# The first norm of a two-model kernel: x over two DMA queues, squares on two engines, the sum over tiles on VectorE

## The reference

```python
def rms_norm(x, g):
    xf = x.astype(F32)
    y = xf * lax.rsqrt(jnp.mean(xf * xf, axis=-1, keepdims=True) + NORM_EPS)
    return (y * g.astype(F32)).astype(x.dtype)

def first_block(x, norm_mix_g, w_in, ...):
    h = x
    for layer in range(DEPTH):
        u = rms_norm(h, norm_mix_g[layer])
        p = u @ w_in[layer]
        p_a, p_b, p_c, p_gate = _split(p, (A_COLS, B_COLS, C_COLS, GATE_COLS))
        ...
```

## Time and profile before

| | us |
|---|---|
| median of three runs | 2533.5 (2531.13 to 2535.11) |
| the profiled execution | 2517.57 |
| its span, first to last instruction | 2516.1 |
| TensorE busy in the span | 2304.6 (92%) |
| VectorE busy | 1596.2 (63%) |
| ScalarE busy | 1178.8 (47%) |

### The profile page before, as it was taken

The page is one execution under the profiler, slowest core; times in us unless marked ns, Lnnn a source line. Parts: engine busy times, 40 slices in busy tenths (PEclk is TensorE's granted clock), DMA queues, the critical chain, the costliest instruction groups (busy, mean ns, idle before and its releaser), DMA issues.

```text
span 2516.1 us, 45037 instructions
## 1 busy us (share of the span) xinstructions
PE 2304.6 (92%) x19087; PEld 2076.5 (83%) x19087; DVE 1596.2 (63%) x2425; ACT 1178.8 (47%) x1717; POOL 0.2 (0%) x4
## 2 busy tenths in 40 slices
PE   7889788899988887988998989999989999999998
PEld 7669788899976777888998979998977788887776
DVE  5537776677763687576775656555654444568886
ACT  5234534455552355355554435445333434456665
POOL 0000000000000000000000000000000000000000
PEclk9999898999999999899998989999987999999999
DMA  5674333355446533253553414554312555569895
GB/s 201 224 257 157 113 106 105 130 183 191 139 173 261 197 118 116 86 175 121 193 192 100 134 59 168 185 190 137 118 34 84 184 176 183 190 237 324 321 330 197
DMA packets 118634, 427.06 MB, mean 170 GB/s; under 512 B 13344, under 2 KB 16160, under 8 KB 118304
## 3 DMA queue, kind: packets, MB, share of 16 engines
q1 hardware_dynamic: 116544, 422.34, 48.9%
q10 hardware_dynamic: 1888, 1.84, 0.2%
HBM read 423.08 MB, written 1.05 MB: 169 GB/s over the span
## 4 chain that ended last, share of the span: by engine, by line
PE 77%; DVE 14%; ACT 4%; issue 2%; DMA 2%; ACTq 0%; SPq 0%; DVEq 0%
PE bank L764 76%; DVE w_low L2176 4%; DVE arena L2208 4%; DMA ring<-in_weights 1%; DVE arena L2217 1%; DVE y_mix L2208 1%; ACT w_high L1672 1%; DVE arena L2678 1%; PE bank L1562 1%; ACT arena L1935 1%; DVE small L2676 0%; DVE arena L2214 0%; DVE arena L2212 0%; DVE arena L2227 0%; ACT arena L1880 0%
## 5 line engine op out<-in xcount | busy, mean ns | idle before, releaser
L2176 DVE TENSOR_TENSOR w_low<-ring,w_high 128x1024 fp32r<-128x1024 f32 x700 | 820.1, 1220 | 146.8 <-ACT w_high L1672 146.7
L764 PE MATMUL bank<-u_high,w_high 128*128 128x256 f32 x2576 | 743.0, 288 | 30.0 <-DVE u_low L2208 23.3
L1672 ACT ACTIVATE w_high<-ring 128x1024 fp32r<-128x1024 f32 x700 | 696.0, 1050 | 134.3 <-PE bank L764 128.0
L764 PE MATMUL bank<-u_low,w_high 128*128 128x256 f32 x2576 | 735.1, 285 | 0.0
L764 PE MATMUL bank<-u_high,w_low 128*128 128x256 f32 x2576 | 734.3, 285 | 0.0
L764 PEld LDWEIGHTS bank<-u_high,w_high 128*128 128x128 f32 x2576 | 499.7, 194 | 42.5 <-issue 39.5
L764 PEld LDWEIGHTS bank<-u_low,w_high 128*128 128x128 f32 x2576 | 499.7, 194 | 0.1
L764 PEld LDWEIGHTS bank<-u_high,w_low 128*128 128x128 f32 x2576 | 498.9, 194 | 0.0
L764 PE MATMUL bank<-arena 64*64 64x64 f32 (+8 forms) x4488 | 258.3, 253 | 78.8 <-DVE arena L2217 22.8
L764 PEld LDWEIGHTS bank<-arena 64*64 64x64 f32 (+3 forms) x4488 | 218.9, 154 | 124.7 <-issue 66.5
L764 PE MATMUL bank<-w_high,u_high 128*128 128x256 f32 (+1 forms) x480 | 166.5, 347 | 5.1 <-DVE w_low L2176 5.1
(11 more groups left out here) (281 smaller groups left out, 3091.1 us busy)
## 6 DMA issues: line engine op xcount, KB each, us to landing
ring<-in_weights SPq DMA_DIRECT2D x534, 512.0 KB, 4.5
ring<-in_moe SPq DMA_DIRECT2D x264, 512.0 KB, 5.3
const<-in_const SPq DMA_DIRECT2D x1, 2619.0 KB, 16.2
x_res<-in_x SPq DMA_DIRECT2D x2, 512.0 KB, 4.8
out<-x_res ACTq DMA_DIRECT2D x2, 512.0 KB, 3.0
const<-in_par ACTq DMA_DIRECT2D x1, 462.0 KB, 3.4
params<-in_par ACTq DMA_DIRECT2D x1, 247.0 KB, 7.9
small<-in_pos SPq DMA_DIRECT2D x1, 128.0 KB, 16.0
```

The lines of the kernel that those rows point to most:

```text
L764: return pe.matmul(out, lhsT, rhs, start=start, stop=stop, skip_group_check=loose)
L1672: act.activation(WH[:, ORDER.slot[cut], :], weights("s", cut), Copy).then_inc(s_hi, 1)
L2176: dve.tensor_tensor(WL[:, b, :], weights("s", cut), WH[:, b, :].bitcast(f32), SUB).then_inc(s_lo, 1)
```

## The change

The first half of x goes out on ScalarE's queue, ahead of `cond`; the second stays first on SyncE's queue. ScalarE squares tiles 0 to 3 in one instruction of 1024 elements a partition, VectorE squares tiles 4 to 7 in one. VectorE adds the two halves (1024 elements), folds the sum twice more (512, 256), and TensorE sums over the partitions with two matmuls instead of 16. The waits for `params` move: on VectorE to behind the low halves of units 0 and 1, on ScalarE to behind the norm. ScalarE cuts the high halves of units 0 and 1 ahead of the root and that of unit 2 behind it. VectorE makes the reciprocal between the low halves of units 1 and 2. The stage has steps of its own (`first`); layer 1 keeps `mix`.

```diff
+    "first_act":
+        "-1 squares root high0 high1 high2 high3 high4 high5 high6 high7",
+    "first_dve":
+        "-3 summed inverse normed0 normed1 low0 normed2 low1 normed3 low2 normed4 low3 normed5 low4 normed6 "
+        "low5 normed7 low6 low7",
...
-            squares_sum(R)
-            pe.wait_ge(s_ident, 16)
+            if layer:
+                squares_sum(R)
+            else:
+                pe.wait_ge(*R.dve("summed"))
+                for h in TWO:
+                    ins = mm(mean_of(R)[:, h:h + 1], sq[:, 0, h * P:(h + 1) * P], mean_weight, True, True)
+                ins.then_inc(*R.pe.mark("sum"))
+                pe.wait_ge(s_ident, 16)
             spread_roots(R)
...
+        def first_squares(R):
+            act.activation(unused, eps, Sqrt).then_inc(*R.act.mark())
+            act.wait_ge(s_x[0], 16)
+            act.activation(sq[:, 0:4, :], X[:, 0:4, :], Square).then_inc(*R.act.mark("squares"))
+            high_to(1)
+            act.wait_ge(*R.pe("sum"))
+            act.activation(rstd[:, :], mean_of(R)[:, 0:2], Sqrt, bias=eps).then_inc(*R.act.mark("root"))
...
+        act.dma_start(X[:, 0:4, :], a_x[0:4].rearrange("k p t -> p k t")).then_inc(s_x[0], 16)
         act.dma_start(cond[:, :], a_cond).then_inc(s_cond, 16)
...
-        act.wait_ge(s_par1, 16)
...
-                squares(R, lambda k: (s_x[k // 4], 16))
+                first_squares(R)
                 high_to(s0 + 2)
...
             rms(R)
+            act.wait_ge(s_par1, 16)
...
             recip(d, rstd[:, :], "inverse")
+            if R is of_mix[0]:
+                low_to(2)
             dve.wait_ge(*R.pe("spread"))
...
+        def first_squares(R):
+            d = R.dve
+            dve.wait_ge(s_x[1], 16)
+            tt(d, sq[:, 4:8, :], X[:, 4:8, :], X[:, 4:8, :], MUL)
+            dve.wait_ge(*R.act("squares"))
+            for n in (4, 2, 1):
+                prior(d)
+                tt(d, sq[:, 0:n, :], sq[:, 0:n, :], sq[:, n:2 * n, :], ADD, "summed" if n == 1 else "-")
...
-        dve.wait_ge(s_par1, 16)
...
-                low_to(s0 + 2)
+                first_squares(R)
+                low_to(1)
+                dve.wait_ge(s_par1, 16)
             rms(R, lambda k: par1(layer, "norm_mix", k))
...
-        for h in TWO:
-            sp.dma_start(X[:, 4 * h:4 * h + 4, :], a_x[4 * h:4 * h + 4].rearrange("k p t -> p k t")).then_inc(s_x[h], 16)
+        sp.dma_start(X[:, 4:8, :], a_x[4:8].rearrange("k p t -> p k t")).then_inc(s_x[1], 16)
```

More of the change, by code:

```diff
@@ L277 @@
         "-2 eps cond",
[L278 to L284, removed]
     "mod_pe":
@@ L339 @@
         "x0 x1 x2 x3 x4 x5 x6 x7",
+    "first_pe":
+        "sum spread",
+    "first_act":
[3 more added lines that the diff above has]
+        "low5 normed7 low6 low7",
+    "mix_pe":
+        "sum spread",
+    "mix_act":
+        "-1 sq0 sq1 sq2 sq3 sq4 sq5 sq6 sq7 root high0 high1 high2 high3 high4 high5 high6 high7",
+    "mix_dve":
+        "inverse normed0 normed1 low0 normed2 low1 normed3 low2 normed4 low3 normed5 low4 normed6 low5 "
+        "normed7 low6 low7",
     "conv_act":
@@ L705, in build @@
     of_start = stage("start", 0)
-    of_mix, of_mod, of_a, of_b, of_c, of_merge, of_ffn, of_add = (
+    of_mod, of_a, of_b, of_c, of_merge, of_ffn, of_add = (
         [stage(name, layer) for layer in range(LAYERS)]
-        for name in ("mix", "mod", "a", "b", "c", "merge", "ffn", "add"))
+        for name in ("mod", "a", "b", "c", "merge", "ffn", "add"))
+    of_mix = [stage("first", 0), stage("mix", 0)]
     of_conv = [[stage("conv", layer * FF_GROUPS + j) for j in range(FF_GROUPS)] for layer in range(LAYERS)]
```

## The result

| | before | after |
|---|---|---|
| median, six runs each | 2534.06 (2530.17 to 2539.52) | 2520.82 (2514.1 to 2526.5) |
| span of the profiled execution | 2516.1 | 2522.7 |
| its mean granted clock | 0.951 | 0.945 |

The ratio of the runs is 0.9946, with a 95% interval of 0.9927 to 0.9964: 9 to 18 us less, where 7.5 were forecast. The two profiled executions stand the other way round, by 6.6 us. Both can be true only if something that has nothing to do with the first norm moves a single execution by several microseconds. Two later measurements of the same pair gave 0.9977 (0.9963 to 0.9991) and 0.9975 (0.9961 to 0.9989), 6 us, and those are my best estimate of the change. The first of the two leaves out two slow ones of its 31 runs of before (2641.56 and 11694.93 us).

A forecast was written before the change was run, and what follows sets the result against it. The kernel was taken as bound by matmuls once they flow. The first normed tile was to move from 23.52 to 16.0, and these 7.5 us to reach the end: 2533.5 - 7.5 = 2526.0 us, range 2520.5 to 2531.5.

The forecast's parts named there:

- The row of the megabyte: Landing of all of x before the change, 6.75 us, used as the neighbour for `cond` landing at 7.0.
- The rest of the sum: Steps from `cond`'s landing at 7.0 to the first normed tile at 16.0: squares, additions, low halves, reciprocal, spread; 9.0 us.
- What is behind: Work after the first norm, such as `omu` on VectorE at 22.2: claimed to let the 7.5 us reach the end whole.
- The slow level: TensorE's first 27 records after the norm at the 1.2 GHz level, 0.22 us each: claimed to take 5.9 us as before.
- The rival of a lasting slow level: TensorE's 240 records after the norm stay slow longer; all slow would lose 21.3 us, 2547.3; chance 0.04.
- the range's last term: Allowance for spread between runs in the end-to-end range: 2 us.
- the slow queue: Rival at the start: ScalarE's queue is served slowly, `cond` lands at 9.7, gain 4.8, 2528.7; chance 0.13 including loss at constants.
- two queues brought x 0.4 us sooner: Rival at the start: x really comes sooner, `cond` lands at 4.75, gain 9.7, 2523.8; chance 0.11.

The follow-up runs named there:

- e3: The changed kernel with `cond` issued ahead of the half of x on ScalarE's queue: ratio to before 0.9972.
- e9: The changed kernel with `cond` first and then both halves of x on ScalarE's queue: one run, 2533.42 us, before 2530.49.
- e1: The changed kernel measured again without any edit, against the kernel before: ratio 0.9977.
- e11: The changed kernel measured a third time without any edit, on another chip, against the kernel before: ratio 0.9975.
- e10: The changed kernel with both halves of x on SyncE's queue and the `params` waits back ahead of the squares: one run, 2525.83 us, before 2530.49.

## Why the prediction came out as it did, point by point

**The mechanism** was right. The wait for `params` left the chain, 4 records stood where 32 were, VectorE's low halves became what is late, and the reciprocal followed the second of them without a wait for `params`.

**`cond`.** Taken as 7.0 from bounds of 4.75 and 8.2; it landed at 7.94. The row of the megabyte (6.75) was the right neighbour for x, which was complete at 6.3, but the turns with the weights' pieces, which I had only in the upper bound, cost 1.6 us (in the stretch from 6.3 to 7.94 ScalarE's queue moved 166 packets and SyncE's 164). This is the whole error at the front: `cond` was 0.9 us late, and the tile came at 16.8 where 16.0 were forecast. The price of a turn, 0.18 us, holds beside pieces of 4 KB (e3, e9), but by luck: it took all 16 pieces an engine of `params` to fall between 6.75 and 9.58, and the trace of before has only 139 packets of ScalarE's queue there, under 9 an engine, beside 277 of SyncE's.

**The rest of the sum.** From `cond` to the end of the square 2.68 forecast and measured; the additions 2.4 and 2.41; low halves 2.36 and 2.35; reciprocal to normed tile 1.54 and 1.54. The root was ready at 14.5, 0.8 us ahead of VectorE (1.2 forecast).

**What is behind.** VectorE came to `omu` at 23.03; the last small load had landed at about 22. TensorE met no gap in its 240 records, as forecast. The slow level lasted as long as before in the profiled execution and in e1. The rival of a lasting slow level is out: with 4 records ahead instead of 32 the products sped up after the same 6 us, and in e11 after 3.0. I took 5.9 us as a fixed length; it isn't one.

**The size and the range.** 7.5 us were forecast; the trace has 6.7 to 7.1 at the front, and the two repeated measurements 5.8 and 6.3. The first one lies outside the range. Its median, 2520.82, would be within 2520.5 to 2531.5, but its six runs of before stood at 2534.06; the ratio 0.9946 on the 2533.5 of the forecast gives 2519.8, a gain of 13.7 where the range ended at 13. The step that failed is the range's last term, the 2 us of spread between runs, which I took from the 4 us between the lowest and highest of three runs of before. The front's own error, 0.8 us less gain than forecast, points the other way. The 87 runs show a standard deviation of 4.4 us, 2518.5 to 2540.8. Two means of six runs then differ by +-5 us by chance (1.96 x 4.4 x the root of 2/6). The first result's means differ by 13.4: 6.1 are the difference of the larger samples (2531.2, 87 runs, and 2525.1, 24 runs), 2.8 that the six runs of before stood above the first mean, 4.5 that the six of the changed kernel stood below the second. With 13.4 against 6.1 this is more than that allows 19 times in 20, so a further cause in that one measurement can't be excluded; it was not seen again. Part of the excess was visible in the mean clock, 0.9457 for the six runs after against 0.9448 for the runs of before, 1.7 us at 1.9 us per 0.001. The profiled executions, 16 us under the median in the case of before, had been the warning: I noted the distance and did not ask what could make it. Why that first measurement stood so far out stays open; the runs show only that two others, with 12 runs after against 29 and 23 before, did not repeat it.

**Of the rivals,** the slow queue was the nearest to what happened, at a third of its price; two queues brought x 0.4 us sooner at the cost of `cond`. The rule of the Trainium skill (DMA: Bandwidth & Descriptors, section Issuing engines are not separate DMA queues) holds in what the runs show: a second queue brought no bandwidth (379 GB/s from 3 to 7 us after, 372 before), and the change would have been better without it. The same page, in the section Queues, rings and completion order, says that a DMA engine goes round its queues a packet at a time; the counts of e9, 396 against 390 and 53 against 51 in spite of the sizes, agree.

**Open** stays what decides where the half-clock stretches fall. The scatter starts with the first products (up to 1.0 us at the exponential) and grows between 75 and 180 us: at the first `y_mix` row of ScalarE the two executions of before stand at 177.91 and 182.24, three of the changed kernel at 175.09, 179.07 and 173.19.

## What to carry to other kernels

A wait written in front of an engine's whole program can hold work that doesn't need it: moving it to its first user brought 4.7 of the 6.7 us at the normed tile for no instruction. A wait in front of an activation can hold its table load too, 1.3 us in e10. A small transfer that the chain starts from belongs in front of its queue, and a large one on the queue where the other large ones wait behind it and not beside it. Where single runs scatter by four microseconds, judge a part of one or two by a fixed point of the trace ahead of the scatter, and take the measurement's width from many runs before a range is given.

## What the runs showed of the hardware

- Of VectorE, a clear of 128x2048 took 1.8 us, and the next began 2.14 us after the one before.
